# Feature products of a feed-forward chunk: eight products with the high half of the weights, then eight with the low half

## The chip, the cores and the metric

The kernel runs on one core of one Trainium2 chip. A core has five engines that run their own instruction lists side by side: TensorE (PE, matrix products), VectorE (DVE), ScalarE (ACT), GpSimd (POOL) and SyncE (SP, which here issues the loads of weights). In the profile TensorE has two rows: PE for the products and PEld for the loads of the stationary operand that belong to them. The metric is the time of one execution in microseconds, lower is better.

## The reference, cut to what matters

The reference is a stack of transformer blocks on 256 tokens of width 1024, in float32: a first block (recurrent and sparse attention mixer, feed-forward), then two blocks of a second kind. Five feed-forward layers of inner width 2816 hold most of the work:

```python
    # first block
    h = rms_norm(x, norm_ffn_pre[l])
    f = (jax.nn.silu(h @ w_ffn_gate[l]) * (h @ w_ffn_up[l])) @ w_ffn_down[l]
    x = x + rms_norm(f, norm_ffn_post[l])
...
def swiglu(h, w_gu, w_down):
    g, u = jnp.split(h @ w_gu, 2, axis=-1)
    return (jax.nn.silu(g) * u) @ w_down
...
        # second block, twice for each of its two layers
        x = x + 0.5 * swiglu(rmsnorm(x, ffn1_norm[l]), ffn1_w_gu[l], ffn1_w_down[l])
```

All of it is computed to nearly float32 accuracy from products of a shorter float type, called fp32r. Each operand is split in a high half and a low half (high = the value rounded to fp32r, low = the rest), and a product of two matrices is the sum of three: high times high, high times low, low times high.

## The kernel before, in words

**Weights.** Every weight matrix is read once, in chunks of 128 x 1024 float32 (512 KB): two slices k of the contraction, 512 columns each. SP loads chunk i into `RAW` (six buffers, `load`). ACT copies it to `WH`, the high half (`hi`, six buffers); before it overwrites a buffer it waits for the semaphore of the last product that read the chunk six places earlier (`final_pass`). DVE subtracts and writes `WL`, the low half (`lo`). ACT works five chunks ahead of PE: while PE is at chunk i, ACT writes chunk i + 5.

**Products.** A `Product` is one block of 512 columns of a weight matrix. `passes` is the list of pairs (chunk, block) in which PE goes through it, and `mm` issues one pair. There are three kinds:

- Most products keep tokens as the stationary operand and stream the weights, 512 columns at a time: three products for each k (lines 361 to 363).
- `features` products without `wide` keep the weights as the stationary operand and stream the activations, 256 tokens at a time: three products for each k (lines 355 to 357). They occur in the first mixer alone.
- `wide` products, in the feed-forward layers, do with two products what takes three otherwise. The high and the low half of the activations lie in one tensor `AT0B[:, half, k, :]`, half 8 KB apart. Line 347 streams both halves, 512 columns in two pieces of 256, against the high half of a 128 x 128 weight tile. Line 349 streams the high half of the activations, 256 columns in one piece, against the low half of the tile, and adds to the left half of the same PSUM bank.

**Feed-forward layer f.** `w_gu` is read as 11 groups of 512 columns (256 of the gate, 256 of the other factor). Groups 0 and 1 are of the first kind. Groups 2 to 10 are `wide`: four tiles of 128 features, one PSUM bank each, four chunks for each group. So a layer has 9 x 4 = 36 wide chunks, and the five layers have 180. Even groups use banks 4 to 7, odd groups banks 0 to 3. After the groups comes the down product (`FT`, first kind, lines 361 to 363).

**Order of PE in a wide chunk.** `pe_group` takes the passes in turn: for each of the four tiles b, for each of the two k, line 347 and then line 349. So 512-column and 256-column products alternate, eight of each in a chunk. Within group 2 six 128 x 128 transposes (line 407) stand after the first chunk and four after the second.

**Who waits for whom.** Before a pass PE waits for `lo` of the chunk. Before the first pass of a group into a bank it waits until that bank's last content has been read (`p.free`: `f_gate` for the first two banks, `f_up` for the other two, both of two groups earlier). At the end of each pass a semaphore `mm` is raised. It is waited for in two places: by ACT before it overwrites the `WH` buffer (the chunk's last pass), and by `act_right` (line 1394), which reads the finished sums, two banks at a time. ACT runs `act_right` for group g - 1 right after the `hi` that stands first in group g.

Of the kernel before, what the change touches and what calls it, by code (L numbers as in the profile page):

```python
# [16 lines left out]
S = 256  # L17
# [4 lines left out]
NHL = 6  # L22
# [38 lines left out]
class Signals:  # L61
# [17 lines left out]
    def on(self, name, key):  # L79
        return self.sems[name], self.value[(name, key)] if self.counted else 1  # L80
# [15 lines left out]

@dataclass
class Product:

# [27 lines left out]
def build(nc, a, out):  # L129
    with ExitStack() as ctx:  # L130
# [8 lines left out]
        AT0B = sb("AT0", [128, 2, 8, S], F32R)  # L139
        AT0 = AT0B[:, 0], AT0B[:, 1]  # L140
        RAW = [sb(f"RAW{i}", [128, CHUNK]) for i in range(NRAW)]
        WH = [sb(f"WH{i}", [128, CHUNK], F32R) for i in range(NHL)]
# [60 lines left out]
        PB = [PX[:, i, :] for i in range(8)]  # L203
# [34 lines left out]
        def product(w, c0, n, src, banks, ks=(0, 8), blocks=0, lead=0, **more):  # L238
            p = Product(w, c0, n, ks[0], ks[1], src, banks, first=len(stream), blocks=blocks, lead=lead, **more)
            kt = min(8, CHUNK // n)  # L240
            for k in range(p.k_lo, p.k_hi, kt):
                p.spans[len(stream)] = (k, min(k + kt, p.k_hi))
                stream.append((w, k, min(kt, p.k_hi - k), c0, n))
            chunks = list(p.spans)
            nb = n // 128 if p.features else 2
            cut = len(chunks) - blocks
            p.passes = [(i, b) for b in range(nb) for i in chunks[:lead]]
            p.passes += [(i, b) for i in chunks[lead:cut] for b in range(nb)]
            p.passes += [(i, b) for b in range(nb) for i in chunks[cut:]]
            return p  # L250
# [73 lines left out]
        def lo(e, i):  # L324
            if i < len(stream):
# [2 lines left out]
                e.tensor_tensor(WL[i % NHL][:, 0:m], RAW[i % NRAW][:, 0:m], WH[i % NHL][:, 0:m].bitcast(F32),  # L328
                                ALU.subtract).then_inc(*up("lo", i))

        def mm(e, p, i, b):

            k0, k1 = p.spans[i]
            h, l = WH[i % NHL], WL[i % NHL]
            e.wait_ge(*on("lo", i))
            bank = p.banks[b // 2 if p.features and not p.wide else b]
            if i == p.first and p.opens:
                for s, key in p.free.get(bank, ()):
                    e.wait_ge(*on(s, key))
            for k in range(k0, k1):  # L340
                kx, j = k ^ p.shift, (k - k0) * p.n
                for s, key in p.need.get((kx, b), ()):
                    e.wait_ge(*on(s, key))
                start, stop = k == p.k_lo and p.opens, k == p.k_hi - 1 and p.closes
                if p.wide:
                    f = slice(j + b * 128, j + b * 128 + 128)
                    e.matmul(PB[bank].rearrange("p (h s) -> p h s", h=2), h[:, f], AT0B[:, :, kx, :], start=start,  # L347
                             stop=False, skip_group_check=True)
                    ins = e.matmul(PB[bank][:, 0:S], l[:, f], p.src[0][:, kx, :], start=False, stop=stop,  # L349
                                   skip_group_check=True)  # L350
                elif p.features:
                    start = start and b % 2 == 0
                    o = PB[bank][:, b % 2 * S:b % 2 * S + S]
                    f = slice(j + b * 128, j + b * 128 + 128)
                    e.matmul(o, h[:, f], p.src[0][:, kx, :], start=start, stop=False, skip_group_check=True)  # L355
                    e.matmul(o, h[:, f], p.src[1][:, kx, :], start=False, stop=False, skip_group_check=True)  # L356
                    ins = e.matmul(o, l[:, f], p.src[0][:, kx, :], start=False, stop=stop, skip_group_check=True)  # L357
                else:
                    o = PB[bank][:, 0:p.n]
                    t = slice(b * 128, b * 128 + 128)  # L360
                    e.matmul(o, p.src[0][:, kx, t], h[:, j:j + p.n], start=start, stop=False)  # L361
                    e.matmul(o, p.src[0][:, kx, t], l[:, j:j + p.n], start=False, stop=False)  # L362
                    ins = e.matmul(o, p.src[1][:, kx, t], h[:, j:j + p.n], start=False, stop=stop)  # L363
            ins.then_inc(*up("mm", (i, b)))
# [1021 lines left out]
        def act_right(e, f, g, i):  # L1386

            rooms, sums = group_rooms(f, g)
            if g < 4:
                e.wait_ge(*on("hT", (f, g - 2)))  # L1390
            else:
                e.wait_ge(*on("f_lo" if i else "f_mult", (f, g - 2)))
            e.wait_ge(*on("mm", F[f][0][g].end(2 * i + 1)))
            e.activation(rooms[i], sums[i][1], ACT.Copy).then_inc(*up("f_right", (f, g, i)))  # L1394

        def dve_gate(e, f, g):
# [627 lines left out]
        def pe_group(e, f, g):  # L2024

            p = F[f][0][g]
            for x, (i, b) in enumerate(p.passes):
                if g == 1 and x < 2 * p.lead:
                    continue
                mm(e, p, i, b)  # L2030
                if g == 2 and x == 3:
                    pe_turn_h(e, f, 0)
                    pe_spread(e, f)
                if g == 2 and x == 7:
                    pe_turn_h(e, f, 1)

        def pe_begin(e, n, p):
# [1527 lines left out]
```

## Time and profile before

| what | us |
|---|---|
| median of 3 runs | 1407.73 |
| lowest, highest | 1406.33, 1409.03 |
| the profiled execution, its own time | 1409.42 |
| its span (first to last instruction) | 1407.6 |
| PE busy in the span | 1385.2 (98%) |
| mean granted clock of TensorE | 0.996 |

The profiled execution's own time is 1.8 us longer than its span, and 1.7 us longer than the median. Busy time of PE has to be read with care. The recorded duration of a product runs until its results are out, and the next one starts long before: products of 398 ns start 235 ns apart. What a product costs is the distance from its start to the start of the next, called its step below. It is read from the timeline.

### The profile page before, as it was taken

Reading aid. Unit: us, or ns where it says so; the run is one execution under the profiler, and the core shown is the slowest. Engines: PE = TensorE matmul, PEld = TensorE weight load, DVE = VectorE, ACT = ScalarE, POOL = GpSimd, SP = SyncE. Lnnn points to the kernel's source line nnn. Section 1 sums busy time; section 2 is a strip of 40 time slices with the busy share of each in tenths; the row PEclk is TensorE's granted clock in tenths of the full one; section 3 lists DMA queues with packets and bytes.
Section 4 is the critical chain, followed back from the end, with each engine's and each line's share of the span. In section 5 each row is a group of like instructions: output and inputs, shape, how many; then the busy total and the mean of one; then the engine's idle time right before and its main releaser. Section 6 shows DMA issues by size and latency. Waiting matters only on the chain.

```text
span 1407.6 us, 19523 instructions
## 1 busy us (share of the span) xinstructions
PE 1385.2 (98%) x7290; PEld 1175.5 (84%) x7290; DVE 967.2 (69%) x1472; ACT 810.4 (58%) x1264; POOL 53.5 (4%) x62
## 2 busy tenths in 40 slices
PE   8999999999999999999999999999999999999999
PEld 7898788788887888888788888888888877888887
DVE  7999856667755676756977777556675584667753
ACT  6679944565645555545866555445554576565541
POOL 2021000000000000000000000000000070000000
PEclk9999999999999999999999999999999999999999
DMA  9544455476555566566346665566655541366651
GB/s 314 173 121 135 153 162 182 133 224 182 191 186 173 177 185 185 189 187 198 110 164 197 185 188 190 185 192 182 181 193 181 160 150 31 121 208 186 190 193 60
DMA packets 127213, 242.64 MB, mean 172 GB/s; under 512 B 7568, under 2 KB 13328, under 8 KB 127120
## 3 DMA queue, kind: packets, MB, share of 16 engines
q1 hardware_dynamic: 126208, 239.15, 55.0%
q0 software_dynamic: 624, 2.10, 0.5%
q8 instruction: 60, 0.98, 0.3%
q14 instruction: 33, 0.27, 0.1%
q10 hardware_dynamic: 288, 0.14, 0.0%
HBM read 240.31 MB, written 1.05 MB: 171 GB/s over the span
## 4 chain that ended last, share of the span: by engine, by line
PE 93%; DVE 4%; ACT 2%; issue 1%; DMA 0%; ACTq 0%; DVEq 0%
PE PX L347 24%; PE PX L361 16%; PE PX L363 16%; PE PX L362 16%; PE PX L349 12%; PE PX L407 3%; PE PX L652 2%; DVE WL L328 1%; PE PX L541 1%; PE PX L355 1%; PE PX L356 1%; PE PX L357 1%; PE PX L545 0%; ACT WH L322 0%; PE PX L1055 0%
## 5 line engine op out<-in xcount | busy, mean ns | idle before, releaser
L328 DVE TENSOR_TENSOR WL<-RAW,WH 128x1024 fp32r<-128x1024 f32 (+2 forms) x454 | 554.7, 1227 | 356.2 <-ACT WH L322 354.0
L322 ACT ACTIVATE WH<-RAW 128x1024 fp32r<-128x1024 f32 (+2 forms) x454 | 477.1, 1054 | 507.6 <-PE PX L363 268.1
L347 PE MATMUL PX<-AT,WH 128*128 128x512 f32 x1440 | 508.1, 398 | 0.0
L349 PE MATMUL PX<-AT,WL 128*128 128x256 f32 x1440 | 403.3, 280 | 0.0
L347 PEld LDWEIGHTS PX<-AT,WH 128*128 128x128 f32 x1440 | 270.5, 188 | 65.9
L349 PEld LDWEIGHTS PX<-AT,WL 128*128 128x128 f32 x1440 | 271.7, 189 | 0.2
L361 PE MATMUL PX<-WH,AT 128*128 128x512 f32 (+4 forms) x528 | 210.7, 399 | 6.4 <-DVE AT L1312 6.0
L363 PE MATMUL PX<-WH,AT 128*128 128x512 f32 (+4 forms) x528 | 201.9, 382 | 0.0
L362 PE MATMUL PX<-WL,AT 128*128 128x512 f32 (+4 forms) x528 | 201.4, 381 | 0.0
L361 PE MATMUL PX<-WH,FTh 128*128 128x512 f32 x440 | 171.6, 390 | 0.0
L363 PE MATMUL PX<-WH,FTl 128*128 128x512 f32 x440 | 171.3, 389 | 0.0
L362 PE MATMUL PX<-WL,FTh 128*128 128x512 f32 x440 | 171.2, 389 | 0.0
L361 PEld LDWEIGHTS PX<-WH,AT 128*128 128x128 f32 x528 | 100.2, 190 | 26.3 <-issue 8.6
L362 PEld LDWEIGHTS PX<-WL,AT 128*128 128x128 f32 x528 | 100.2, 190 | 18.8 <-issue 2.2
L363 PEld LDWEIGHTS PX<-WH,AT 128*128 128x128 f32 x528 | 99.7, 189 | 19.1
L363 PEld LDWEIGHTS PX<-WH,FTl 128*128 128x128 f32 x440 | 82.6, 188 | 17.3
L361 PEld LDWEIGHTS PX<-WH,FTh 128*128 128x128 f32 x440 | 82.6, 188 | 17.1
L362 PEld LDWEIGHTS PX<-WL,FTh 128*128 128x128 f32 x440 | 82.6, 188 | 17.0
L1394 ACT ACTIVATE SR<-PX 128x512 f32<-128x512 f32 x90 | 48.0, 585 | 0.0
L355 PE MATMUL PX<-AT,WH 128*128 128x256 f32 x128 | 37.9, 296 | 0.0
L356 PE MATMUL PX<-AT,WH 128*128 128x256 f32 x128 | 36.1, 282 | 0.0
L357 PE MATMUL PX<-AT,WL 128*128 128x256 f32 x128 | 36.1, 282 | 0.0
(333 smaller groups left out, 1327.9 us busy)
## 6 DMA issues: line engine op xcount, KB each, us to landing
RAW<-in_ffn_w_gu_dram SPq DMA_DIRECT2D x132, 512.0 KB, 3.7
RAW<-in_ffn_w_gu_2b_dram SPq DMA_DIRECT2D x88, 512.0 KB, 3.7
RAW<-in_w_in_dram SPq DMA_DIRECT2D x44, 512.0 KB, 3.7
RAW<-in_ffn_w_down_dram SPq DMA_DIRECT2D x44, 512.0 KB, 3.3
RAW<-in_ffn_w_down_2b_dram SPq DMA_DIRECT2D x44, 512.0 KB, 3.3
RAW<-in_w_ffn_down_dram SPq DMA_DIRECT2D x22, 512.0 KB, 3.6
RAW<-in_ev_w_in_dram SPq DMA_DIRECT2D x20, 512.0 KB, 3.6
RAW<-in_w_rnn_out_dram SPq DMA_DIRECT2D x8, 512.0 KB, 3.7
```

Of the source, the lines that this page charges most:

```text
L322: e.activation(WH[i % NHL][:, 0:m], RAW[i % NRAW][:, 0:m], ACT.Copy).then_inc(*up("hi", i))
L328: e.tensor_tensor(WL[i % NHL][:, 0:m], RAW[i % NRAW][:, 0:m], WH[i % NHL][:, 0:m].bitcast(F32), ALU.subtract).then_inc(*up("lo", i))
L347: e.matmul(PB[bank].rearrange("p (h s) -> p h s", h=2), h[:, f], AT0B[:, :, kx, :], start=start, stop=False, skip_group_check=True)
L349: ins = e.matmul(PB[bank][:, 0:S], l[:, f], p.src[0][:, kx, :], start=False, stop=stop, skip_group_check=True)
L355: e.matmul(o, h[:, f], p.src[0][:, kx, :], start=start, stop=False, skip_group_check=True)
L356: e.matmul(o, h[:, f], p.src[1][:, kx, :], start=False, stop=False, skip_group_check=True)
L357: ins = e.matmul(o, l[:, f], p.src[0][:, kx, :], start=False, stop=stop, skip_group_check=True)
L361: e.matmul(o, p.src[0][:, kx, t], h[:, j:j + p.n], start=start, stop=False)
L362: e.matmul(o, p.src[0][:, kx, t], l[:, j:j + p.n], start=False, stop=False)
L363: ins = e.matmul(o, p.src[1][:, kx, t], h[:, j:j + p.n], start=False, stop=stop)
L407: ins = e.transpose(PB[bank][0:s.shape[1], j * 128:j * 128 + 128], s, ID[:, :])
L1394: e.activation(rooms[i], sums[i][1], ACT.Copy).then_inc(*up("f_right", (f, g, i)))
```

## The change

In a wide chunk PE first issues all eight products with the high half (four tiles, two k each, 512 columns), then all eight with the low half (256 columns). The list of passes has two entries for a chunk in place of four. The high pass waits for `hi` and for the banks, the low pass for `lo`. Each of the two raises `mm` once, so the semaphore is raised twice in a chunk, no longer four times. Accordingly `act_right` waits for the end of the group's last low pass for both halves (`end(1)`), and the indices after which the transposes of group 2 stand go from 3 and 7 to 1 and 3.

```diff
-            nb = n // 128 if p.features else 2
+            nb = n // 128 if p.features and not p.wide else 2
...
+        def mm_wide(e, p, i, low):
+
+            k0, k1 = p.spans[i]
+            w = (WL if low else WH)[i % NHL]
+            e.wait_ge(*(on("lo", i) if low else on("hi", i)))
+            for t, bank in enumerate(p.banks):
+                if i == p.first and not low:
+                    for s, key in p.free.get(bank, ()):
+                        e.wait_ge(*on(s, key))
+                for k in range(k0, k1):
+                    f = slice((k - k0) * p.n + t * 128, (k - k0) * p.n + t * 128 + 128)
+                    if low:
+                        ins = e.matmul(PB[bank][:, 0:S], w[:, f], p.src[0][:, k, :], start=False, stop=k == p.k_hi - 1,
+                                       skip_group_check=True)
+                    else:
+                        ins = e.matmul(PB[bank].rearrange("p (h s) -> p h s", h=2), w[:, f], AT0B[:, :, k, :],
+                                       start=k == p.k_lo, stop=False, skip_group_check=True)
+            ins.then_inc(*up("mm", (i, low)))
+
         def mm(e, p, i, b):
 
             k0, k1 = p.spans[i]
             h, l = WH[i % NHL], WL[i % NHL]
+            if p.wide:
+                mm_wide(e, p, i, b)
+                return
...
-                if p.wide:
-                    f = slice(j + b * 128, j + b * 128 + 128)
-                    e.matmul(PB[bank].rearrange("p (h s) -> p h s", h=2), h[:, f], AT0B[:, :, kx, :], start=start,
-                             stop=False, skip_group_check=True)
-                    ins = e.matmul(PB[bank][:, 0:S], l[:, f], p.src[0][:, kx, :], start=False, stop=stop,
-                                   skip_group_check=True)
-                elif p.features:
+                if p.features:
...
-            e.wait_ge(*on("mm", F[f][0][g].end(2 * i + 1)))
+            e.wait_ge(*on("mm", F[f][0][g].end(1)))
...
-                if g == 2 and x == 3:
+                if g == 2 and x == 1:
                     pe_turn_h(e, f, 0)
                     pe_spread(e, f)
-                if g == 2 and x == 7:
+                if g == 2 and x == 3:
                     pe_turn_h(e, f, 1)
```

PE's list of instructions at the head of group 4 or later of a layer, before: `WH4` and `WL4` are the two halves of one chunk, `AT0` the activations, and a wait stands behind the row that has it.

```order
2503 L347 MATMUL PX<-AT0,WH4 128x512 [waits s_f_gate,s_lo]
2504 L349 MATMUL PX<-AT0,WL4 128x256
2505 L347 MATMUL PX<-AT0,WH4 128x512
2506 L349 MATMUL PX<-AT0,WL4 128x256
2507 L347 MATMUL PX<-AT0,WH4 128x512 [waits s_f_up,s_lo]
2508 L349 MATMUL PX<-AT0,WL4 128x256
2509 L347 MATMUL PX<-AT0,WH4 128x512
2510 L349 MATMUL PX<-AT0,WL4 128x256
2511 L347 MATMUL PX<-AT0,WH4 128x512 [waits s_f_up,s_lo]
2512 L349 MATMUL PX<-AT0,WL4 128x256
2513 L347 MATMUL PX<-AT0,WH4 128x512
2514 L349 MATMUL PX<-AT0,WL4 128x256
```

The same place of a group now (the low products have line 344, `WH0` and `WL0` are a chunk's halves, `x7` stands for seven equal rows):

```order
1401 L347 MATMUL PX<-AT0,WH0 128x512 [waits s_f_gate,s_hi]
1402 L347 MATMUL PX<-AT0,WH0 128x512
1403 L347 MATMUL PX<-AT0,WH0 128x512 [waits s_f_gate]
1404 L347 MATMUL PX<-AT0,WH0 128x512
1405 L347 MATMUL PX<-AT0,WH0 128x512 [waits s_f_up]
1406 L347 MATMUL PX<-AT0,WH0 128x512
1407 L347 MATMUL PX<-AT0,WH0 128x512 [waits s_f_up]
1408 L347 MATMUL PX<-AT0,WH0 128x512
1409 L344 MATMUL PX<-AT0,WL0 128x256 [waits s_lo]
1410 L344 MATMUL PX<-AT0,WL0 128x256 x7
1411 L347 MATMUL PX<-AT0,WH1 128x512 [waits s_hi]
1412 L347 MATMUL PX<-AT0,WH1 128x512 x7
```

The sixteen products of a chunk are the same, their order is another, and the waits for the last two banks (`s_f_up`) come after four and six products where they came after eight and twelve. Nothing else moves on PE.

ACT's list around the read of a group's sums, in the kernel before: line 322 is `hi`, line 1394 the read, and the `s_mm` of `WH3` is the last pass of the chunk that held that buffer, which is the last chunk of the group that is read.

```order
290 L1429 ACTIVATE FTh<-SR 128x512 [waits s_f_mult]
291 L322 ACTIVATE WH3<-RAW3 128x1024 [waits s_mm,s_d_w3]
292 L1394 ACTIVATE SR<-PX 128x512 [waits s_mm,s_f_mult]
293 L1394 ACTIVATE SR<-PX 128x512 [waits s_mm,s_f_lo]
294 L322 ACTIVATE WH4<-RAW4 128x1024 [waits s_mm,s_d_w4]
```

This piece is the same after the change but for the value that the first line 1394 waits for. The lists of DVE, SP and POOL are the same too.

## Rows read from the trace of the kernel before

**Rows 1.** The page: chain by line; groups: xcount, busy us, mean ns
```profile
PE PX L347 24%; PE PX L361 16%; PE PX L363 16%; PE PX L362 16%; PE PX L349 12%; PE PX L407 3%; PE PX L652 2%; DVE WL L328 1%; PE PX L541 1%; PE PX L355 1%; PE PX L356 1%; PE PX L357 1%; PE PX L545 0%; ACT WH L322 0%; PE PX L1055 0%
...
L347 PE MATMUL PX<-AT,WH 128*128 128x512 f32 x1440 | 508.1, 398 | 0.0
L349 PE MATMUL PX<-AT,WL 128*128 128x256 f32 x1440 | 403.3, 280 | 0.0
```

**Rows 2.** Waits of PE: longest first: total us, times, longest us
```profile
PE PX L361 <- DVE AT L1312: 6.0, 2, 3.3
```

**Rows 3.** The five wide stretches, one for each feed-forward layer, as windows
```profile
core 0: us, PE busy (x) PEld busy (x) DVE busy (x) ACT busy (x) POOL busy (x), PEclk, DMA share, GB/s
290.29:393.07 102.78, 102.78 (x588) 89.35 (x586) 72.45 (x91) 58.90 (x76) 0.00 (x0) 1.00 0.63 192
481.26:584.04 102.78, 102.78 (x588) 89.32 (x587) 70.43 (x80) 56.24 (x73) 0.00 (x0) 1.00 0.63 189
763.81:866.61 102.80, 102.80 (x588) 89.38 (x586) 72.78 (x97) 56.24 (x73) 0.00 (x0) 1.00 0.63 193
950.06:1052.86 102.80, 102.80 (x588) 89.30 (x587) 70.42 (x80) 56.24 (x73) 0.00 (x0) 1.00 0.62 185
1243.44:1344.41 100.97, 100.97 (x587) 88.41 (x586) 70.80 (x81) 56.30 (x73) 0.00 (x0) 1.00 0.64 196
```

**Rows 4.** Timeline of PE, first wide stretch: start us, recorded duration us, line
```profile
304.39 0.40 PE L347 MATMUL PX<-AT,WH 128*128 128x512 f32 x1
304.63 0.28 PE L349 MATMUL PX<-AT,WL 128*128 128x256 f32 x1
304.74 0.40 PE L347 MATMUL PX<-AT,WH 128*128 128x512 f32 x1
...
305.80 0.40 PE L347 MATMUL PX<-AT,WH 128*128 128x512 f32 x1
```

**Rows 5.** Timeline of PE, fifth wide stretch, four pairs apart
```profile
1289.29 0.40 PE L347 MATMUL PX<-AT,WH 128*128 128x512 f32 x1
...
1290.67 0.40 PE L347 MATMUL PX<-AT,WH 128*128 128x512 f32 x1
```

**Rows 6.** Timeline of PE, a down product, 512 columns, eight steps apart
```profile
599.74 0.39 PE L361 MATMUL PX<-WH,FTh 128*128 128x512 f32 x1
...
601.55 0.39 PE L363 MATMUL PX<-WH,FTl 128*128 128x512 f32 x1
```

**Rows 7.** Timeline of PE, first mixer: first 256-column products after 512-column ones
```profile
63.57 0.28 PE L355 MATMUL PX<-AT,WH 128*128 128x256 f32 x1
...
64.52 0.28 PE L357 MATMUL PX<-AT,WL 128*128 128x256 f32 x1
...
65.48 0.28 PE L356 MATMUL PX<-AT,WH 128*128 128x256 f32 x1
```

**Rows 8.** Timeline of PE: 512-column products right after a row of 256-column ones
```profile
124.92 0.40 PE L361 MATMUL PX<-WH,AT 128*128 128x512 f32 x1
...
126.76 0.39 PE L363 MATMUL PX<-WH,AT 128*128 128x512 f32 x1
```

**Rows 9.** Timeline of PE: the first wide product of a layer, after 512-column ones
```profile
290.29 0.39 PE L347 MATMUL PX<-AT,WH 128*128 128x512 f32 x1
290.52 0.28 PE L349 MATMUL PX<-AT,WL 128*128 128x256 f32 x1
```

**Rows 10.** Loads of the stationary operand, line 355: duration ns minimum, median, maximum
```profile
L355 PEld LDWEIGHTS PX<-AT,WH x128: 187/192/193, 63.3 to 124.4; 128*128 128x128 f32 x128
```

**Rows 11.** Timeline of DVE: last read of group 2's sums, first layer
```profile
307.94 0.68 DVE L1413 TENSOR_TENSOR SR<-PX,SR 128x512 f32<-128x512 f32 x1
```

**Rows 12.** Timeline of PE: 512-column products after 264-column ones
```profile
24.30 0.39 PE L361 MATMUL PX<-WH,AT 128*128 128x512 f32 x1
...
25.21 0.39 PE L362 MATMUL PX<-WL,AT 128*128 128x512 f32 x1
```

**Rows 13.** A stretch at the lower clock, as a window; columns as in rows 3
```profile
456.00:460.00 4.00, 3.02 (x7) 2.47 (x8) 3.65 (x17) 1.84 (x7) 0.00 (x0) 0.59 0.72 252
```

More of the change, by code:

```diff
@@ L334, in mm @@
             h, l = WH[i % NHL], WL[i % NHL]
+            if p.wide:
+                mm_wide(e, p, i, b)
+                return
             e.wait_ge(*on("lo", i))
-            bank = p.banks[b // 2 if p.features and not p.wide else b]
+            bank = p.banks[b // 2 if p.features else b]
             if i == p.first and p.opens:
```

## The prediction, before the kernel was run

> **What bounds the kernel now.** I read the page first, and of it the chain. It runs nearly all the way through PE's product lines, 24% of the span on line 347 and 12% on line 349, the two that the change reorders [rows 1]. Then the waits of PE: the longest is 6.0 us in all, for a step between layers, and neither line 347 nor 349 stands in that view [rows 2]. So in the wide stretches PE waits for nobody, and only what a product costs PE can move the time. The five stretches as windows show the same: PE is busy throughout, DVE for 70%, ACT for 57%, the DMA engines for 63%, at the full clock of 2.4 GHz (granted clock 1.00) [rows 3]. The stretches take 102.78, 102.78, 102.80, 102.80 and 100.97 us, together 512.1 us. The fifth does the same work in 1.8 us less, with no difference in waits. That is the first hint that the cost of a product depends on more than its own size.
>
> The mean durations of 398 and 280 ns [rows 1] overlap and are not costs. The costs are steps, read in the timeline. In the first stretch a high product takes 0.24 us (304.39 to 304.63) and a low one 0.11 to 0.12; four pairs last 1.41 us, a pair 0.353 [rows 4]. In the fifth stretch four pairs last 1.38 us, a pair 0.346 [rows 5]. Where 512-column products follow each other, eight steps last 1.81 us, 0.226 each [rows 6]. Where 256-column products do, eight steps last 0.96 us, 0.120 each (64.52 to 65.48) [rows 7]. A settled 512 and a settled 256 are together 0.346: exactly the pair of the fifth stretch. So alternation as such is not slow. It has a slow rhythm, 7 ns above the sum of the settled steps, which four stretches of five are in, and a fast one.
>
> **The change, part by part.** *Order of the sixteen products.* The chunk becomes a row of eight 512s and a row of eight 256s. If both rows were settled, it would take 1.81 + 0.96 = 2.77 us. But each row begins right after the other kind, and the trace shows what that does. 256s after 512s: the first eight steps last 0.95 us (63.57 to 64.52), a touch less than settled [rows 7]. 512s after settled 256s: the first eight steps last 1.84 us (124.92 to 126.76), 0.03 more than settled [rows 8]. Both rows settle within the eight steps, so this pair of transitions can repeat from chunk to chunk. That gives 1.84 + 0.95 = 2.79 us for a chunk, against 8 x 0.353 = 2.83 in the slow rhythm and 2.77 in the fast one.
>
> The sum: a stretch is 36 chunks plus what its ten transposes add. The fifth stretch gives this addition: 100.97 - 36 x 2.773 = 1.13 us, where 2.773 is eight fast pairs of 0.3467 (the 1.38 us of four pairs, refined by 0.2267 + 0.12). The new stretch is 36 x 2.79 + 1.13 = 101.6 us, five are 508.0, and 512.1 - 508.0 = 4.1 us are gained. Four stretches gain 1.2 us each less rounding (102.8 to 101.6), the fifth loses 0.6: 4.8 - 0.6 = 4.2, the same within rounding. The down product after each stretch starts with a few slow steps in either order; I leave 0.1 us for it.
>
> *Two pieces of 256 columns.* All 512s of rows 6 and 8 stream one piece, line 347 streams two. Is its longer step its own, or its neighbour's doing? The first wide product of a layer, which still follows 512s, goes 290.29 to 290.52: 0.23, the step of a one-piece product, and it does so in all five layers [rows 9]. So I take the pieces at nothing. The lower bound is nothing, the upper bound is the slow step 0.236 kept by all eight.
>
> *Loads of the stationary operand.* They take 187 to 193 ns, longer than the 120 ns step of a 256-column product [rows 10], yet 128 of line 355 with as many of 356 and 357 run at that step [rows 7]. So a row of low products does not wait for them: cost nothing. The Trainium skill, "TensorE: Matmul & The Clock Gate", section "The mechanism" of Part 3, says that such a load overlaps with products in flight only when it goes to other rows of the array. By that the low row would take at least 8 x 0.188 = 1.50 us rather than 0.95, and the change would lose 0.55 us a chunk, about 100 us in all. The rows contradict it, so it gets no chance of its own.
>
> *Waits.* The high pass needs `hi` alone, the low pass `lo`; both are ready chunks ahead, since PE never waits there [rows 2]. The waits for the last two banks come up to 2 us earlier within a group's first chunk. Behind a late one all of PE would queue. In the first layer the last read of group 2 ends at 308.6 us [rows 11]; group 4, the next in these banks, starts eight chunks and 1.0 us of transposes after 290.3, at about 313.9. The cover is 5 us, so nothing. Two semaphore raises fewer in a chunk: nothing, a raise has no step of its own. `act_right` waits for the group's end for both halves. In ACT's queue it stands behind the `hi` that already waits for the same last pass, so it starts when it did: nothing. The buffers of `WH` come free at the end of a chunk as before. A chunk shorter by 0.04 us leaves ACT at 57% and DVE at 70% with room, and the loads at 63%.
>
> *Sum.* 4.2 us less. The profiled execution would go from 1409.4 to 1405.2. Its excess of 1.7 us over the median I carry along unchanged: 1407.7 - 4.2 = 1403.5. A caution: the runs before differ by 2.7 us, and a stretch in the slow rhythm rather than the fast one is 1.8 us. If the median run has one more fast stretch than the profiled one, the gain against it is 1.8 us smaller.
>
> **The rivals.** *Both rows settle at once.* 512s after 264-column products show no slow start: four steps last 0.91 us (24.30 to 25.21), 0.227 each [rows 12]. Then a chunk is 2.77, the stretch 36 x 2.773 + 1.13 = 101.0, five 504.9, a gain of 7.3: 1400.4. Against it stand rows 8, the nearer case with its 256 columns.
>
> *The rhythm stays.* The steps depend on what came before in a way that I read off two transitions only. The chunk may fall in a rhythm of its own at 2.81 to 2.83 us, as alternation did. Then five stretches last 5 x (36 x 2.81 + 1.13) = 511.5 to 5 x (36 x 2.827 + 1.13) = 514.5 us: from 0.6 less to 2.4 more, 1407.1 to 1410.1. For it: alternation has two rhythms with no visible reason. Against it: both new rows are seen to settle.
>
> *Length alone counts.* The Trainium skill, "TensorE: Matmul & The Clock Gate", section "Back-to-back issue gap", gives the step as columns / 2.4 plus 2.5 ns, 216 and 109 ns, whatever stands before. In this kernel that would be a step that belongs to the product: the same sixteen in any order, 1407.7. Against it: the same pair lasts 0.353 and 0.346 us [rows 4, 5].
>
> *Slower: the long step belongs to the two pieces.* If a 512 in two pieces costs 0.236 whenever another follows it, the chunk is 8 x 0.236 + 0.95 = 2.84, because the 256s no longer give back the short steps (0.116) that they have behind a slow 512. Five stretches: 5 x (36 x 2.84 + 1.13) = 516.8, 4.7 more: 1412.4. It is slower from a step of 0.233 on (8 x 0.233 + 0.95 = 2.81, the present average). For it: a two-piece 512 followed by another was never seen. Against it: rows 9.
>
> *The clock.* After gaps between layers PE runs at 1.2 GHz for a while: the window 456 to 460 has a granted clock of 0.59 for seven products [rows 13]. There are three such places before the last product. Each costs about six products x 0.2 us, 1.2 us. Layers that start a microsecond earlier could gain or lose one: 1.2 us either way, widening every case.
>
> **How the numbers follow.** Forecast 2.79 us a chunk: 47%, 1403.5. Both rows settled: 16%, 1400.4. Rhythm of 2.81 to 2.83: 20%, centre 1408.6. Length alone: 6%, 1407.7. Two pieces: 11%, 1412.4. This kernel's measurement can tell about 0.2%, 2.8 us, from no change: 1404.9 to 1410.5 counts as the same. The forecast's own spread (1402 to 1406, with the clock and the caution above) lies for three quarters on the faster side. Faster: 36 + 16 + 3 = 55%. Same: 11 + 15 + 6 + 2 = 34%. Slower: 2 + 9 = 11%. The range leaves out the two-piece case and the ends of the others: 1399.6 to 1409.8.
>
> **What would show it.** Chunk length in the five stretches (windows): 101.6 us each, all alike, if I am right; 101.0 for instant settling, 102.3 and more for a rhythm, 103.4 for the two pieces. In the timeline the high steps should start at 0.233 to 0.236 and fall to 0.227 by the sixth, the low ones at 0.114 and then 0.120. Eight equal high steps of 0.235 would prove the two pieces. Waits of PE on lines 347 or 344, or idle time before `act_right`, would show that I was wrong about the waits. I am wrong altogether if high steps vary with the chunk in no fixed pattern.

## The result, and the profile after

| | before | after |
|---|---|---|
| median of 20 runs, us | 1408.99 | 1405.79 |
| lowest, highest | 1406.33, 1410.38 | 1403.09, 1409.62 |
| profiled execution: own time | 1409.42 | 1404.55 |
| its span, mean granted clock | 1407.6, 0.996 | 1402.7, 0.998 |

The change is faster by a little: the ratio is 0.9979 with a 95% interval of 0.9973 to 0.9986, which is 3.0 us; the two medians differ by 3.2. The chain of the changed kernel runs through the same lines as before [rows 1]; line 344 has the low products now, lines 378 to 380 are what 361 to 363 were. The first line is the chain by line, the next three are groups (count, busy us, mean ns, idle us before), the last of them `act_right`, which was line 1394 before:

```profile
PE PX L347 24%; PE PX L378 16%; PE PX L380 16%; PE PX L379 16%; PE PX L344 12%; PE PX L424 3%; PE PX L669 2%; PE PX L558 1%; DVE WL L329 1%; PE PX L372 1%; PE PX L374 1%; PE PX L373 1%; PE PX L562 0%; ACT WH L323 0%; DMA X<-in_x_dram 0%
...
L347 PE MATMUL PX<-AT,WH 128*128 128x512 f32 x1440 | 361.3, 393 | 0.0
...
L344 PE MATMUL PX<-AT,WL 128*128 128x256 f32 x1440 | 200.8, 282 | 0.0
...
L1411 ACT ACTIVATE SR<-PX 128x512 f32<-128x512 f32 x90 | 48.1, 585 | 0.0
```

The two busy times fell from 508.1 + 403.3 to 361.3 + 200.8 us [rows 1], which is not a gain of 349 us. Equal products in a row overlap, and the page counts the overlap once. The five wide stretches as windows tell what the work costs (window, length, busy time of each engine, granted clock, DMA share, GB/s; [rows 3] are those of before):

```profile
core 0: us, PE busy (x) PEld busy (x) DVE busy (x) ACT busy (x) POOL busy (x), PEclk, DMA share, GB/s
290.92:392.54 101.62, 101.62 (x588) 89.57 (x586) 72.40 (x91) 58.92 (x76) 0.00 (x0) 1.00 0.64 194
479.20:580.84 101.64, 101.64 (x588) 89.58 (x586) 70.38 (x80) 56.26 (x73) 0.00 (x0) 1.00 0.64 193
760.56:862.20 101.64, 101.64 (x587) 89.57 (x586) 72.72 (x97) 56.26 (x73) 0.00 (x0) 1.00 0.64 194
945.65:1047.28 101.63, 101.63 (x588) 89.58 (x586) 70.38 (x80) 56.26 (x73) 0.00 (x0) 1.00 0.63 188
1237.85:1339.49 101.64, 101.64 (x587) 89.57 (x586) 70.82 (x81) 56.27 (x73) 0.00 (x0) 1.00 0.64 194
```

All five are 101.6 us, where before four were 102.8 and one 101.0. Their sum is 508.2 us against 512.1: 3.9 us gained in the trace. One chunk in the timeline of PE (start, duration until the last result, line; x8 is a row of eight):

```profile
303.15 2.00 PE L347 MATMUL PX<-AT,WH 128*128 128x512 f32 x8
304.99 1.12 PE L344 MATMUL PX<-AT,WL 128*128 128x256 f32 x8
305.94 0.40 PE L347 MATMUL PX<-AT,WH 128*128 128x512 f32 x1
```

The high row takes 304.99 - 303.15 = 1.84 us, the low row 305.94 - 304.99 = 0.95 us, the chunk 2.79. The signs that the prediction named are there: the steps of this high row are 0.233, 0.236, 0.228, 0.233, 0.230 and from the sixth on 0.227 us, those of the low row 0.114, 0.119 and then 0.120. Nothing new waits: the idle time before lines 347, 344 and `act_right` is 0.0, and the longest wait of PE within the work is still this one, of [rows 2]:

```profile
PE PX L378 <- DVE AT L1329: 6.0, 2, 3.3
```

The span fell by 4.9 us, 1.0 more than the stretches. That last microsecond is the clock. At two places ahead of wide stretches PE is idle for some 3 us (6.0 us together in the line above), and may run a while at 1.2 GHz behind it. Around the first such gap both kernels show the same granted clock (0.86, the first line of each pair), around the second only before does (the second lines, 0.86 in the first pair, which is before, and 1.00 in the second, the change):

```profile
262.00:274.00 12.00, 8.75 (x40) 6.85 (x39) 10.25 (x28) 8.37 (x27) 0.00 (x0) 0.86 0.46 144
452.00:464.00 12.00, 9.26 (x38) 7.16 (x37) 10.54 (x25) 6.56 (x18) 0.00 (x0) 0.86 0.56 173
```
```profile
262.00:274.00 12.00, 8.74 (x39) 6.86 (x38) 10.60 (x27) 8.21 (x26) 0.00 (x0) 0.86 0.45 138
452.00:464.00 12.00, 9.26 (x48) 7.37 (x47) 10.21 (x25) 7.42 (x23) 0.00 (x0) 1.00 0.56 175
```

The second gap lies between the first and the second wide stretch. From the end of the one to the start of the other, before takes 481.26 - 393.07 = 88.2 us and the change 479.20 - 392.54 = 86.7. That is 1.5 us gained. Against it stand 0.6 us lost ahead of the first stretch, which starts at 290.92 and not at 290.29. Other runs bear the price out: this piece takes 88.1 us with the start by twos (granted clock 0.86 in the same window) and 89.5 with rows of sixteen (0.72).

### The profile page after: what moved, and what is told of

Same layout as the page of the kernel before. It is cut to its first block, busy times and chain, and to the rows that moved or that the text cites. A ratio compares the mean times of both kernels' runs of the same rounds, so it can differ in the third digit from the quotient of the medians.

```text
span 1402.7 us, 19388 instructions
## 1 busy us (share of the span) xinstructions
PE 1380.0 (98%) x7290; PEld 1177.4 (84%) x7290; DVE 967.4 (69%) x1472; ACT 811.2 (58%) x1264; POOL 53.6 (4%) x62
## 4 chain that ended last, share of the span: by engine, by line
PE 93%; DVE 4%; ACT 2%; issue 1%; DMA 0%; SPq 0%; ACTq 0%; DVEq 0%
PE PX L347 24%; PE PX L378 16%; PE PX L380 16%; PE PX L379 16%; PE PX L344 12%; PE PX L424 3%; PE PX L669 2%; PE PX L558 1%; DVE WL L329 1%; PE PX L372 1%; PE PX L374 1%; PE PX L373 1%; PE PX L562 0%; ACT WH L323 0%; DMA X<-in_x_dram 0%
## 5 line engine op out<-in xcount | busy, mean ns | idle before, releaser
L347 PE MATMUL PX<-AT,WH 128*128 128x512 f32 x1440 | 361.3, 393 | 0.0
L347 PEld LDWEIGHTS PX<-AT,WH 128*128 128x128 f32 x1440 | 259.2, 189 | 46.6
L344 PEld LDWEIGHTS PX<-AT,WL 128*128 128x128 f32 x1440 | 196.4, 190 | 14.1
L344 PE MATMUL PX<-AT,WL 128*128 128x256 f32 x1440 | 200.8, 282 | 0.0
L374 PE MATMUL PX<-AT,WL 128*128 128x256 f32 x128 | 36.2, 283 | 0.0
```

The costliest lines, as they stand in the source:

```text
L344: ins = e.matmul(PB[bank][:, 0:S], w[:, f], p.src[0][:, k, :], start=False, stop=k == p.k_hi - 1, skip_group_check=True)
L347: ins = e.matmul(PB[bank].rearrange("p (h s) -> p h s", h=2), w[:, f], AT0B[:, :, k, :], start=k == p.k_lo, stop=False, skip_group_check=True)
```

## The experiments

The theory to test: in the wide stretches a product's step depends on the products before it. A settled row of 512s steps by 0.2267 us, a settled row of 256s by 0.120, and a change from 256 to 512 costs some slow steps; the change of the kernel gains because it has one such change in a chunk and settles in between. The rivals: the gain is that of fewer waits and raises; the long steps belong to the two-piece operand; the bank matters. A chunk's time below is worked out from its stretch as (stretch - 1.13) / 36, with the 1.13 us for transposes of the prediction.

### Before once more

No edit.

> The kernel before, unchanged, profiled once more: which rhythm do its five wide stretches fall in? Theory (a 256-column product followed by a 512-column one sets the following steps, and how a stretch begins decides between two rhythms): each stretch is either 102.8 us or 101.0 us long, nothing between, and the mix may differ from the first trace (four long, one short). Rival (the short fifth stretch has a cause in that layer, its loads or its neighbours): again four of 102.8 us and the fifth of 101.0 us.

Windows of the five stretches:

```profile
291.06:393.89 102.83, 102.83 (x587) 89.38 (x586) 72.42 (x91) 58.91 (x76) 0.00 (x0) 1.00 0.64 192
482.21:584.99 102.78, 102.78 (x588) 89.36 (x586) 70.40 (x80) 56.25 (x73) 0.00 (x0) 1.00 0.63 189
764.78:867.57 102.79, 102.79 (x587) 89.31 (x586) 72.74 (x97) 56.26 (x73) 0.00 (x0) 1.00 0.64 192
951.04:1052.01 100.97, 100.97 (x587) 88.37 (x586) 70.33 (x80) 56.31 (x73) 0.00 (x0) 1.00 0.63 189
1240.86:1341.83 100.97, 100.97 (x588) 88.44 (x586) 70.77 (x81) 56.30 (x73) 0.00 (x0) 1.00 0.64 196
```

The same program now has three long and two short stretches, 510.3 us in all where the first trace had 512.1 [rows 3]. So the alternating order has two rhythms, and the fourth stretch took the one in the first execution and the other in this one. Both traces agree in the two lengths to 0.05 us. The fifth stretch is short in both, so that it may have a cause of its own; but it can't be that layer alone, since the fourth was short too.

### Few waits and one raise a chunk, the order of before

```diff
+            e.wait_ge(*on("hi", i))
+            e.wait_ge(*on("lo", i))
             for t, bank in enumerate(p.banks):
...
+                for k in range(k0, k1):
+                    e.matmul(..., h[:, f], AT0B[:, :, k, :], ...)
+                    ins = e.matmul(..., l[:, f], p.src[0][:, k, :], ...)
+            ins.then_inc(*up("mm", (i, 0)))
```

> The other half of the change alone: order of products as before (512, 256, 512, 256 ...), but one wait for hi and lo and one raise of mm for a chunk, where before there were four of each. Theory (order alone costs): the stretches stay at 102.8 or 101.0 us. Rival (the gain came from fewer waits and raises): all stretches near 101.6 us, a chunk 2.79 us.

The sum of the five windows (length, busy time of each engine):

```profile
sum 512.12, PE 512.12 PEld 445.81 DVE 356.75 ACT 283.98 POOL 0.00; mean PE 102.42 PEld 89.16 DVE 71.35 ACT 56.80 POOL 0.00
```

512.12 us, against 512.13 for the five windows of before, four long and one short in both. One raise in place of four and two waits for `hi` and `lo` in place of four for `lo` are worth nothing here, down to 0.01 us in 512. The rival falls: what is left of the change is the order.

### Rows of sixteen, and the change on the same chip

```diff
-            p.passes += [(i, b) for i in chunks[lead:cut] for b in range(nb)]
+            p.passes += [(i, b if not p.wide or x % 2 == 0 else 1 - b) for x, i in enumerate(chunks[lead:cut]) for b in range(nb)]
...
```

(with the read of a group's sums waiting for its last pass).

> The change taken further: every second chunk does its low products first and then its high ones, so that rows of sixteen 512s and sixteen 256s follow each other, and a chunk has half as many changes from 256 to 512. Theory (a pair of changes costs 0.020 us, settled steps are 0.2267 and 0.120): a chunk 2.773 + 0.010 = 2.783 us on average, a stretch 36 x 2.783 + 1.13 = 101.3 us, five 506.6 us, 1.6 us less than with the change, some 5 us less than before. Rival (waits count, not order): no difference to the change, 101.6 us. Rival (longer rows do not settle into the same steps): above 101.6 us.

> The changed kernel as it is, on the same chip as the variant with rows of sixteen, for the comparison: stretches of 101.6 us each, all five alike; time about 0.998 of the kernel before. If its rhythm depended on how a stretch begins, as with the alternating order, some stretch would differ from 101.6 us by 0.5 us or more.

The sum of the five windows with rows of sixteen, then these rows in PE's timeline:

```profile
sum 506.62, PE 506.62 PEld 448.03 DVE 356.62 ACT 284.21 POOL 0.00; mean PE 101.32 PEld 89.61 DVE 71.32 ACT 56.84 POOL 0.00
```
```profile
306.06 2.08 PE L344 MATMUL PX<-AT,WL 128*128 128x256 f32 x16
307.97 3.82 PE L347 MATMUL PX<-AT,WH 128*128 128x512 f32 x16
311.63 0.76 PE L344 MATMUL PX<-AT,WL 128*128 128x256 f32 x5
```

506.6 us, as the theory said to 0.1 us. The sixteen 512s take 311.63 - 307.97 = 3.66 us, which is 16 x 0.2267 + 0.03: the slow steps at the head are paid once for sixteen, where the change pays them for each eight. The sixteen 256s take 1.91 = 16 x 0.120 - 0.01. The change itself repeated its stretches of 101.6 us, 508.2 in all. In time the rows of sixteen have 0.9961 of before (0.9949 to 0.9972), the change 0.9981 (0.9972 to 0.9989) on the same chip.

### One piece in place of two

```diff
-        AT0B = sb("AT0", [128, 2, 8, S], F32R)
-        AT0 = AT0B[:, 0], AT0B[:, 1]
+        AT0B = sb("AT0", [128, 8, 2, S], F32R)
+        AT0 = AT0B[:, :, 0], AT0B[:, :, 1]
...
-                        ins = e.matmul(PB[bank].rearrange("p (h s) -> p h s", h=2), w[:, f], AT0B[:, :, k, :],
+                        ins = e.matmul(PB[bank][:, :], w[:, f], AT0B[:, k, :, :].rearrange("p h s -> p (h s)"),
...
```

> As the changed kernel, but the high and the low half of the activations lie side by side for each k, so that line 347 streams 512 columns in one piece. Theory (two pieces cost nothing): chunk 2.793 us and stretches of 101.6 us as with the change. Rival (part of the long steps 0.233 to 0.236 at the head of a row of 512s belongs to the two pieces): chunk 2.773 us or nearer to it, stretches 101.0 us.

The sum of the five windows:

```profile
sum 508.20, PE 508.20 PEld 447.87 DVE 356.57 ACT 283.97 POOL 0.00; mean PE 101.64 PEld 89.57 DVE 71.31 ACT 56.79 POOL 0.00
```

508.20 against 508.17 us. The two pieces cost nothing, and the rival that would have made the change slower is out.

### Rows of two

```diff
                     e.matmul(..., h[:, f], AT0B[:, :, kx, :], ...)
+                    if k < k1 - 1:
+                        continue
+                    for q in range(k0, k1):
+                        ...
+                        ins = e.matmul(..., l[:, f], p.src[0][:, q, :], ...)
```

> One size changed: in each tile both 512-column products and then both 256-column ones, rows of two in place of one (before) and eight (the change); waits and raises as in the kernel before. Theory (each change from 256 to 512 and back costs up to 0.020 us until settled, four such pairs a chunk, not settled within two steps): between 2.773 and 2.853 us a chunk, stretches of 101.0 to 103.8 us, in one or more rhythms that a chunk length in steps of 0.0133 us shows. Rival (the cost belongs to the number of products, not of changes): 2.79 us as with rows of eight.

The sum of the five windows, each of them 101.42 to 101.44 us:

```profile
sum 507.14, PE 507.14 PEld 443.22 DVE 356.58 ACT 283.95 POOL 0.00; mean PE 101.43 PEld 88.64 DVE 71.32 ACT 56.79 POOL 0.00
```

All five are 101.4 us, a chunk of 2.786. That is inside what I expected, and only 0.2 us a stretch from the rival's 101.6 (all five lie within 0.02 us, so the difference is real), but it takes a part of the theory away: with four changes from 256 to 512 in a chunk it costs less than the rows of eight with one. So the cost is not a fixed price for each change. In the timeline the eight products of two rows of each kind repeat every 1.39 us:

```profile
304.36 0.63 PE L347 MATMUL PX<-AT,WH 128*128 128x512 f32 x2
304.83 0.39 PE L353 MATMUL PX<-AT,WL 128*128 128x256 f32 x2
305.05 0.63 PE L347 MATMUL PX<-AT,WH 128*128 128x512 f32 x2
305.52 0.40 PE L353 MATMUL PX<-AT,WL 128*128 128x256 f32 x2
305.75 0.63 PE L347 MATMUL PX<-AT,WH 128*128 128x512 f32 x2
```

A pair of 512s takes 0.47 us both times, but the pair of 256s takes 0.22 and then 0.23 us, shorter than the settled 0.24, and the settled pair of 512s would take 0.45. Short rows gain a little at the 256s and lose a little at the 512s.

### 264 columns in the low products

```diff
-                        ins = e.matmul(PB[bank][:, 0:S], w[:, f], p.src[0][:, k, :], ...)
+                        ins = e.matmul(PB[bank][:, 0:264], w[:, f], AT0B.rearrange("p h k s -> p (h k s)")[:, k * S:k * S + 264], ...)
```

> As the changed kernel, but every low product streams 264 columns, not 256 (the eight more are the next slice's values added into columns that belong to the low half's sum, so the output is not the reference's; work is added, none removed). The rows of before show that 264-column products also step by 0.120 us on average and that 512s after them begin at 0.227 without slow steps. Theory (what costs is the phase in which a row of 256s hands over to the 512s, and 264 columns hand over in another): chunk below 2.793 us, down to 2.773, stretches 101.0 to 101.5 us although more columns are streamed. Rival (time follows columns): 64 columns more a chunk at 2.4 columns per ns are 0.027 us, chunk 2.82 us, stretches 102.6 us.

The sum of the five windows, then a chunk in PE's timeline:

```profile
sum 512.18, PE 512.18 PEld 452.58 DVE 356.73 ACT 283.86 POOL 0.00; mean PE 102.44 PEld 90.52 DVE 71.34 ACT 56.77 POOL 0.00
```
```profile
308.99 1.99 PE L347 MATMUL PX<-AT,WH 128*128 128x512 f32 x8
310.82 1.15 PE L344 MATMUL PX<-AT,WL 128*128 128x264 f32 x8
311.80 0.40 PE L347 MATMUL PX<-AT,WH 128*128 128x512 f32 x1
```

My expectation fell: 512.2 us, 4.0 more than the change, close to what the columns alone would add (2.814 us a chunk; the rival said 2.82). Neither of the two readings behind it held. In [rows 12] the 512s after 264s step by 0.227 us from the first on; here the row begins with 0.234, 0.233 and 0.231 and takes 1.83 us, 0.01 less than the 1.84 after 256s and 0.02 more than a settled one. And the 264-column row takes 0.98 us, 0.1225 each, not the 0.120 that I had read off the first mixer. In [rows 12] only six products of 264 columns stand ahead of the 512s, and no 512s ahead of them; here eight do, behind a row of 512s. A step read in one surrounding need not hold in another.

### Five starts for the alternating order

```diff
+def chunk_order(f, g, c):
+    if g == 2 and c == 2 and f < 4:
+        return (rows_of(8), rows_of(2), rows_of(4), rows_of(8, "LH"))[f]
+    return rows_of(1)
...
```

`f` is the layer, `g` the group, `c` the chunk of the group. `rows_of(n)` is the order in rows of n high and n low products, with `"LH"` the low ones first. This kernel and the next three wait and raise as the one with few waits.

> Alternating order everywhere, as before, but in layers 0 to 3 the third chunk of group 2 (the first after the last transposes) is in another order: layer 0 rows of eight, layer 1 rows of two, layer 2 rows of four, layer 3 eight low ones first and then eight high ones. Layer 4 is as before, all alternating. Theory (the steps just before decide, for the whole stretch, which rhythm the alternation keeps): some of the four stretches are short, 101.0 us (chunks of 2.773 us), others long, 102.8 us (chunks of 2.827), and nothing in between from the fifth chunk on, although 34 of 36 chunks are alike in all. Rival (the long rhythm is the natural one and a start cannot change it): all four long. Rival (chance, such as loads of weights at that moment): a rhythm that changes in the middle of a stretch.

The five windows:

```profile
290.81:393.56 102.75, 102.75 (x587) 89.38 (x586) 72.42 (x91) 58.89 (x76) 0.00 (x0) 1.00 0.64 193
481.82:582.82 101.00, 101.00 (x587) 88.43 (x586) 70.34 (x80) 56.31 (x73) 0.00 (x0) 1.00 0.65 193
762.50:865.27 102.77, 102.77 (x587) 89.39 (x586) 72.73 (x97) 56.25 (x73) 0.00 (x0) 1.00 0.64 193
948.69:1051.44 102.75, 102.75 (x587) 89.28 (x586) 70.40 (x80) 56.24 (x73) 0.00 (x0) 1.00 0.62 186
1241.60:1342.57 100.97, 100.97 (x588) 88.36 (x586) 70.76 (x81) 56.30 (x73) 0.00 (x0) 1.00 0.65 196
```

Only layer 1, which starts with a chunk in rows of two, became short; the other three starts gave the long rhythm; layer 4 has no special start and was short by itself, as in every trace of the alternating order so far. One execution with one short stretch more does not prove that the start did it, since a stretch can turn short by itself, as the fourth did in before once more. The last experiment decides.

### Five shapes of rows

```diff
+def chunk_order(f, g, c):
+    if f == 0:
+        return rows_of(4)
+    if f == 1:
+        return rows_of(4, back=True)
+    if f == 2:
+        return rows_of(1, back=True)
+    if f == 3:
+        return rows_of(2, back=True)
+    return rows_of(8, tiles=[(t, k) for k in range(2) for t in range(4)])
...
```

`back` turns every second pair of rows round. In layers 1 and 3 some banks are then opened by a low product that does not clear them, so that their sums are not the reference's; the products issued are the same.

> Five orders of the same sixteen products, one for each layer's wide stretch: layer 0 rows of four; layer 1 rows of four with every second pair turned round (four high, eight low, four high); layer 2 single products turned round (one high, two low, one high); layer 3 two high, four low, two high; layer 4 rows of eight as in the change, but all four tiles of the first k and then of the second, so that products that follow each other go to different banks. Theory (only changes between 256 and 512 columns cost, and the bank does not count): layer 4 has 2.793 us a chunk as the change. The others lie between 2.773 and 2.85, in steps of 0.0067 us; by 0.010 us for each change pair left unsettled, as rows of two measured 2.787 with four pairs, rows of four (two pairs) would be about 2.78 to 2.81. Rival (bank of the product before counts): layer 4 differs from 2.793 us.

The five windows:

```profile
292.19:394.25 102.06, 102.06 (x587) 89.38 (x586) 72.41 (x91) 58.91 (x76) 0.00 (x0) 1.00 0.64 194
480.94:582.61 101.67, 101.67 (x588) 89.50 (x586) 70.34 (x80) 56.24 (x73) 0.00 (x0) 1.00 0.64 192
762.35:863.78 101.43, 101.43 (x588) 88.62 (x587) 72.72 (x97) 56.24 (x73) 0.00 (x0) 1.00 0.65 195
947.18:1049.28 102.10, 102.10 (x588) 89.31 (x587) 70.37 (x80) 56.22 (x73) 0.00 (x0) 1.00 0.62 187
1239.77:1341.41 101.64, 101.64 (x587) 89.59 (x586) 70.80 (x81) 56.26 (x73) 0.00 (x0) 1.00 0.64 195
```

Layer 4, rows of eight over different banks, is at the 101.64 of the change: whether the next product goes to the same bank or to another does not count. Layer 2 (one, two, one: in the stream rows of two) is at the 101.43 of rows of two. Layer 3 (two, four, two: rows of four in the stream) is with layer 0 (rows of four), 102.10 and 102.06. Layer 1 (four, eight, four: rows of eight) is with the change, 101.67. So from rows of two on, the length of the rows in the stream decides, to 0.04 us a stretch. Rows of four rest on these two stretches alone, the other lengths on five or more. These are the prices:

| rows in the stream | stretch, us | chunk, us | where |
|---|---|---|---|
| 1 | 102.8 or 101.0 | 2.824 or 2.773 | before, twice; fewer waits |
| 2 | 101.4 | 2.786 | rows of two; here layer 2 |
| 4 | 102.1 | 2.804 | here layers 0 and 3 |
| 8 | 101.6 | 2.792 | the change, one piece; here layers 1 and 4 |
| 16 | 101.3 | 2.783 | rows of sixteen |

Read from start to start in the timelines, the chunks are 2.827 or 2.773, 2.787, 2.807, 2.793 and on average 2.784 us: the 1.13 us come from the short rhythm, and the formula is up to 0.003 us low for the others.

### Starting the alternation with rows of two

```diff
+def chunk_order(f, g, c):
+    return rows_of(2 if g == 2 and c == 2 else 1)
...
```

and in a second kernel `c in (2, 3)`.

> Alternating order as before, but the third chunk of group 2 of every layer goes in rows of two, which made layer 1 of the kernel with five starts short. Theory (the steps before decide the rhythm, and rows of two lead into the short one): all five stretches 101.0 us, together 505.0 us, 3.2 us less than the change and 5 to 7 us less than before, where two to four of the five stretches were long; time about 0.996 of before. Rival (layer 1 was short by luck, as layers 3 and 4 are in some runs of before): a mix of 102.8 and 101.0 us, no better than before.

> The same with the third and the fourth chunk of group 2 in rows of two. Theory (rows of two reach one fixed cycle within a chunk, and the alternation takes its rhythm from there): the same in all five stretches, each 101.0 us. Rival (it depends on where in the cycle the rows of two end, or on what stood before them): stretches that differ, or all of 102.8 us.

Windows of the first kernel, and the sum of the second:

```profile
292.15:393.13 100.98, 100.98 (x587) 88.39 (x586) 72.37 (x91) 58.98 (x76) 0.00 (x0) 1.00 0.64 196
481.26:582.25 100.99, 100.99 (x587) 88.41 (x586) 70.34 (x80) 56.31 (x73) 0.00 (x0) 1.00 0.64 194
761.95:862.96 101.01, 101.01 (x587) 88.45 (x586) 72.67 (x97) 56.31 (x73) 0.00 (x0) 1.00 0.64 196
946.38:1047.43 101.05, 101.05 (x587) 88.45 (x586) 70.35 (x80) 56.32 (x73) 0.00 (x0) 1.00 0.63 188
1239.11:1340.09 100.98, 100.98 (x587) 88.45 (x586) 70.78 (x81) 56.31 (x73) 0.00 (x0) 1.00 0.64 196
```
```profile
sum 505.11, PE 505.11 PEld 442.25 DVE 356.48 ACT 284.21 POOL 0.00; mean PE 101.02 PEld 88.45 DVE 71.30 ACT 56.84 POOL 0.00
```

Ten stretches of ten are short, in two kernels (100.98 to 101.06 us). Without that start it was one of five (before), two of five (before once more) and one of five (fewer waits): always the last layer's, once the fourth, and in the first three layers none of nine. In those layers it is now six of six, so luck is no explanation any more: the products before the alternation decide its rhythm, and rows of two lead into the short one. Rows of eight, of four, and eight low ones first had not, in one stretch each. The five stretches take 505.0 us, 3.2 less than with the change. The time is 1403.6 against 1408.76 us, ratio 0.996 (0.9947 to 0.9973). This beats before, and its stretches beat the change's; between the rows of sixteen (0.9961) and this one the timing cannot tell. Its profiled execution still has a span of 1403.3 us, more than the 1402.7 of the change, because it ran longer at 1.2 GHz (granted clock 0.994 against 0.998). The first stretch starts 1.2 us later than with the change, and the pieces ahead of the second and of the fifth are 1.5 and 1.1 us longer. Around the first gap it has:

```profile
262.00:274.00 12.00, 8.75 (x32) 6.64 (x31) 9.62 (x25) 7.79 (x24) 0.00 (x0) 0.72 0.46 137
```

In this window both before and the change show 0.86 in their profiled executions; the products in it are the same ones in all three. Taken at equal mean clock, 0.998, the times are 1404.6 us for the change (median of eight runs; seven on another chip have 1404.2) and 1400.4 and 1400.8 for this one (two runs, on a third chip), some 4 us less, of which the stretches give 3.2.

## Why the prediction was right, and where it was off

**Bound and hint.** PE was the bound and the fifth stretch the clue, as read. The chunk came out at 2.79 us, the stretch at 101.62 to 101.64 where 101.6 stood, the five together at 508.2 where 508.0 stood. The two transitions of [rows 7] and [rows 8] repeated from chunk to chunk, step by step as there: 1.84 and 0.95 us, also on average over all 180.

**Two pieces, loads, waits.** All were put at nothing and are: one piece changes 0.03 us in 508, the waits and raises 0.01 in 512. Rows of low products run at the step of 0.120 with loads of 187 to 192 ns, so that these loads stay hidden. That the earlier waits for banks are covered by 5 us was argued from one layer; the idle time of 0.0 before lines 347 and 344 bears it out for all. The waits for the last two banks moved by less than the prediction's "up to 2 us": four high products take 0.93 us where eight alternating ones took 1.41, and six take 1.39 where twelve took 2.12, so they come 0.5 and 0.7 us earlier. (The list of before starts at the chunk's second bank, its fifth product.)

**Rivals.** Instant settling would have needed 101.0 us, the two pieces 103.4, length alone an unchanged stretch. The rival of a rhythm of its own at 2.81 did not occur for rows of eight, but it was a fair one: rows of four come to 2.80, or 2.81 read from start to start. The rival of instant settling rested on [rows 12], and with rows of 264 columns in the wide stretches even these showed slow first steps.

**What was off is the passage from the trace to the median.** The prediction was 1403.5; measured were 1405.8. 1.3 us of the 2.3 are the level of before itself, 1407.73 from three runs and 1408.99 from twenty. The other 1.0 is the gain: 4.2 us against the profiled execution, 3.2 between the medians. The gain is a property of the change minus a property of before that changes from run to run. The trace of before had four long stretches of five, the second one three; against the latter the change gains 510.3 - 508.2 = 2.1 us in the stretches. The prediction named this caution (1.8 us for each short stretch) and gave it no weight in the likeliest time. How often before has one, two or more short stretches was not counted, so that the 1.0 us is assigned to them by argument; the time at the lower clock moves the medians as well. The spans of the unprofiled runs speak for both. On the chip of the rows of sixteen, among runs with the same mean clock of 0.998, the seven of before have spans from 1402.6 to 1406.7 us, the seven of the change from 1402.0 to 1403.0. A spread of 4.1 against 1.0 us is what about two stretches changing rhythm would make, at 1.8 us each. Their medians there are 1406.4 and 1402.4, 4.0 us apart, where all runs together have 3.4.

**The clock term** was right in kind and too narrow. One place at the lower clock cost 1.5 us rather than 1.2, and a layer that starts earlier is not what decides: the granted clock already differs around the first gap, where the kernels are still the same. The rest of the span (span less stretches) is 895.5 us before and 894.5 after, but 896.7 with rows of sixteen and 898.3 with the start by twos, which have the lowest granted clock (0.994). The other runs fit in: 894.6 to 894.9 at 0.997 and 0.998, 894.8 to 895.7 at 0.996, 896.6 to 897.4 at 0.995. All of these run the same products there.

**What stays open.** What sets the two rhythms, and why rows of four are dearer than rows of two and of eight, no run shows. The prices of the table are measured; no formula for them is. Open as well is why the fourth layer's stretch is long in one execution of before and short in the next, and why the last layer's is short in all four traces without a start of its own and the first three layers' never: what differs just ahead of them was not shifted by a known amount in any kernel here.

## What to carry to other kernels

In stretches like these, where TensorE is busy throughout, the cost of a product is the distance to the next start, and here it depended on the products before it: read it in the timeline, per chunk, and compare stretches that do the same work, since a stretch that is 2% faster than its twins shows what is to be had. Orders of the same products can be priced before they are built, if both changes between kinds occur somewhere in the trace from a settled row and the new rows are long enough to settle again; a price read off a few products in another surrounding (264 columns here) did not carry. Ask of a gain of a few parts in a thousand how much the kernel before varies by the very thing that is removed, since the difference of the medians is less than that of one pair of traces.

## What the runs showed of the hardware that I had not expected

The same alternation of 512 and 256 columns has two stable rhythms, 2.82 and 2.77 us a chunk, and kept whichever it fell into for 100 us, over all waits and raises. One or two chunks in rows of two at the start select the short one, in ten stretches of ten; three other orders there did not, in one stretch each. The cost of rows is not monotonic in their length (2.773 or 2.824, 2.786, 2.804, 2.792, 2.783 us for rows of 1, 2, 4, 8, 16). And the time that PE spends at 1.2 GHz after the same idle gap differs between executions: granted clock 0.86 or 0.72 over the same 12 us around the first gap. Over all such places it is worth up to 4 us of the whole (894.5 to 898.3 us outside the stretches), more than the change.
